# Four late modulation blocks of a two-layer transformer: summed by GpSimd instead of multiplied by TensorE

## The chip, the cores and the metric

The kernel runs on one core of a Trainium2 chip. Its engines are TensorE (PE: matmuls, PEld: its weight loads), VectorE (DVE), ScalarE (ACT), GpSimd (POOL) and SyncE (SP), which here does nothing but start transfers. Each engine takes its own instructions strictly in the order of its program and waits for the others by semaphores. The metric is the device time of one execution in microseconds (us). Times of single instructions are those of the hardware profile.

## What is computed

A stack of two layers over 256 tokens of width 1024, all in float32. Layer 0 mixes with differential attention (8 heads, 256 tokens and 256 context tokens as keys), layer 1 with windowed means; behind each mixer stands a mixture of 32 experts. Both layers are steered by a modulation vector:

```python
c_act = jax.nn.silu(c)
for i in range(DEPTH):
    mod = (c_act @ ada_w[i] + ada_b[i])[:, None, :]
    sh1, s1, g1, sh2, s2, g2 = jnp.split(mod, N_MOD, axis=-1)
    h = modulate(rms_norm(x, norm1_g[i]), sh1, s1)
    ...
    x = x + g1 * y
    h2 = modulate(rms_norm(x, norm2_g[i]), sh2, s2)
    out = moe(h2.reshape(-1, D), router_w, router_b, w_gate[i], w_up[i], w_down[i])
    x = x + g2 * out.reshape(B, L, D)
```

`ada_w` is 2 x 1024 x 6144, so the twelve products of the 1024-vector `c_act` with 1024 x 1024 blocks read 48 MB. Block `i` (0 to 11) is part `i % 6` of layer `i // 6`; blocks 8 to 11 are g1, sh2, s2 and g2 of layer 1, which nothing needs before layer 1's mixer has ended.

## The kernel before

The program is written out by hand, engine by engine, with semaphores; there is no scheduler. The stages around the change, with their times in the profile:

- Blocks 0 and 1 are multiplied by TensorE. Then come ten projections `proj(0)` to `proj(9)` (k, q, v of attention, 16 matmuls each), up to 208 us.
- During them VectorE sums blocks 2 to 7 (`accumulate`, L1120 and L1122): a 4 MB block lies in one of three 32 KB-per-partition buffers, `unit(0)` to `unit(2)`, and eight instructions on 128x1024 add up row k times `c_act[k]`, first one `TENSOR_SCALAR`, then seven `SCALAR_TENSOR_TENSOR`, each linked to the next by a semaphore. TensorE adds over the partitions afterwards (`ada_fin`: eight products of one column, L482, or two of 512 columns with a matrix of ones, L485), at places in the projections that `fin_at` sets: block 6 inside `proj(8)`, block 7 inside `proj(9)`. VectorE takes the result up in `mod_use` and raises `mod_used`.
- Attention runs from 208 to 310 us over 16 units `u` (8 heads times 2 halves of the tokens). Per unit TensorE makes the scores of unit u+2 (L552), transposes the weights of u (L605, `w_ready`) and multiplies them with the values of u-1 (L581); VectorE takes the maxima (L1206, L1207), and mixes the two softmaxes (L1215, L1216, L1219); ScalarE takes the exponentials (L876), copies the transposed weights (L920) and scales the output twice (L910, L913). After every fourth unit VectorE forms a mean square (`squares`, L1225), GpSimd its inverse root (`inverse_root`, a power, L397), VectorE scales the four outputs (`normalise`, L1231, in its program just ahead of the end of u = 5, 9, 13 and after 15), TensorE turns them (`turn_outputs`, L563) and at the end multiplies with `w_out` (`project_outputs`, L587).
- Inside that loop, at u = 0, 2, 6 and 8 (`ADA_AT`), TensorE also multiplies blocks 8 to 11: `ada_mm` (L455, 16 matmuls), with a copy by ScalarE (`mod_copy`, L844) and the fold one unit later (`ada_fin`, L473 or L475).
- SyncE's queue is one list. `load_ada` (L303) brings a block in two halves of 512 columns, `load_rows` (L309) in two halves of 512 rows, so that four k of eight are complete in each. Block 8 is requested when the q projections have freed `unit(1)`, blocks 9 to 11 as TensorE frees a unit, then the weights of experts 0, 2 and 1.
- The experts of layer 0 begin with the first weights at about 362 us and set the pace from there by their loads and matmuls; all that lies behind 310 us follows the last `project_outputs`.

## Time and profile before

| | us |
|---|---|
| three runs | 1396.83, 1392.2, 1397.91; median 1396.83 |
| profiled execution: its own time | 1396.81 |
| profiled execution: span | 1395.0 |
| PE busy (share of the span) | 1231.1 (88%) |
| DVE busy | 390.5 (28%) |
| ACT busy | 214.0 (15%) |
| POOL busy | 70.0 (5%) |
| attention, first transposes to last projection | 210.72 to 310.25 |

The span is the time from the first to the last recorded instruction; 1.8 us lie around it. Busy times overlap and don't add up to the span. For a change inside one stage the shares over the whole program say little: what counts is what the engines wait for in that stage.

### The profile page before, as it was taken

Reading aid. Unit: us, or ns where it says so; the run is one execution under the profiler, and the core shown is the slowest. Engines: PE = TensorE matmul, PEld = TensorE weight load, DVE = VectorE, ACT = ScalarE, POOL = GpSimd, SP = SyncE. Lnnn points to the kernel's source line nnn. Section 1 sums busy time; section 2 is a strip of 40 time slices with the busy share of each in tenths; the row PEclk is TensorE's granted clock in tenths of the full one; section 3 lists DMA queues with packets and bytes.
Section 4 is the critical chain, followed back from the end, with each engine's and each line's share of the span. In section 5 each row is a group of like instructions: output and inputs, shape, how many; then the busy total and the mean of one; then the engine's idle time right before and its main releaser. Section 6 shows DMA issues by size and latency. Waiting matters only on the chain.

```text
span 1395.0 us, 13695 instructions
## 1 busy us (share of the span) xinstructions
PE 1231.1 (88%) x5044; PEld 517.5 (37%) x5048; DVE 390.5 (28%) x834; ACT 214.0 (15%) x449; POOL 70.0 (5%) x86
## 2 busy tenths in 40 slices
PE   4899998885999999798989879679999999898996
PEld 2355444444433333232323257353333333332332
DVE  2665645625321121111111033351111111111112
ACT  3211116611111110100101111111110101001000
POOL 0122100000000000000000000000000000000000
PEclk9999999997999999999999989789999999999999
DMA  9956759443699999999999993537999999999994
GB/s 351 404 203 241 281 202 380 193 199 166 268 421 422 422 422 421 422 422 422 421 421 421 419 380 132 230 120 311 421 422 423 421 422 421 422 422 422 421 422 193
DMA packets 84288, 486.54 MB, mean 349 GB/s; under 512 B 6176, under 2 KB 7712, under 8 KB 35104
## 3 DMA queue, kind: packets, MB, share of 16 engines
q1 hardware_dynamic: 82240, 481.91, 84.7%
q10 hardware_dynamic: 2016, 4.21, 0.9%
q8 instruction: 20, 0.33, 0.1%
q14 instruction: 12, 0.10, 0.0%
HBM read 485.04 MB, written 1.05 MB: 348 GB/s over the span
## 4 chain that ended last, share of the span: by engine, by line
PE 56%; DMA 17%; SPq 14%; DVE 7%; issue 2%; ACT 2%; POOL 1%; another core or an unknown queue 0%; DVEq 0%; POOLq 0%; ACTq 0%
PE PS L678 19%; DMA ring<-in_moe_w_up 14%; PE PS L697 10%; SPq L289 10%; PE PS L527 7%; PE PS L705 4%; SPq L294 3%; DMA ring<-in_ada_w 3%; PE PS L789 2%; PE PS L670 2%; PE PS L807 2%; PE PS L587 2%; PE PS L455 1%; DVE ring L1122 1%; POOL stat L397 1%
## 5 line engine op out<-in xcount | busy, mean ns | idle before, releaser
L678 PE MATMUL PS<-ring,KQH 128*64 128x512 f32 x2048 | 482.7, 615 | 34.3 <-DMA ring<-in_moe_w_up 32.6
L678 PEld LDWEIGHTS PS<-ring,KQH 128*64 128x64 f32 x2048 | 147.2, 141 | 314.9 <-issue 276.8
L697 PE MATMUL PS<-ring,KQH 128*64 128x512 f32 x1024 | 230.7, 592 | 0.9 <-ACT KQH L980 0.9
L1443 DVE COPY TMP<-PS 64x512 f32<-64x512 f32 x64 | 43.8, 684 | 470.8 <-PE PS L697 470.8
L527 PE MATMUL PS<-ring,KQH 128*128 128x512 f32 x320 | 143.0, 604 | 1.5 <-DVE KQH L1139 1.5
L697 PEld LDWEIGHTS PS<-ring,KQH 128*64 128x64 f32 x1024 | 73.7, 137 | 147.1 <-issue 145.7
L705 PE MATMUL PS<-TMP,KQH 128*128 128x512 f32 x256 | 118.4, 605 | 1.6 <-DVE TMP L1443 1.6
L967 ACT COPY TMP<-PS 64x512 f32<-64x512 f32 x64 | 37.2, 582 | 466.4 <-PE PS L697 466.4
L1458 DVE TENSOR_TENSOR KQH<-KQH,PS 128x256 f32<-128x256 f32 x64 | 38.7, 605 | 196.3 <-ACT KQH L986 196.3
L527 PEld LDWEIGHTS PS<-ring,KQH 128*128 128x128 f32 x320 | 61.3, 194 | 75.6 <-issue 72.7
L410 POOL COPY KQH<-KQH 128x512 f32 x62 | 38.2, 616 | 873.5 <-PE PS L678 775.9
L705 PEld LDWEIGHTS PS<-TMP,KQH 128*128 128x128 f32 x256 | 46.0, 189 | 73.6 <-issue 70.3
L1428 DVE TENSOR_SCALAR rope_g<-const,route 128x128 f32<-128x128 f32 x128 | 36.3, 346 | 80.8 <-PE PS L688 80.8
L688 PE MATMUL PS<-const,KQH 128*128 128x128 f32 x128 | 26.3, 287 | 35.8 <-DVE KQH L1458 35.8
L1122 DVE SCALAR_TENSOR_TENSOR ring<-ring,ccols 128x1024 f32<-128x1024 f32 x42 | 54.0, 1285 | 5.6 <-DMA ring<-in_ada_w 4.2
L980 ACT COPY KQH<-PS 128x512 f32<-128x512 f32 x64 | 30.7, 479 | 150.7 <-PE PS L688 150.7
L397 POOL TENSOR_TENSOR stat<-stat,mhalf 128x16 f32<-128x16 f32 (+3 forms) x18 | 31.5, 1752 | 404.9 <-DVE stat L1266 144.0
L986 ACT ACTIVATE KQH<-PS 128x256 f32<-128x256 f32 x62 | 23.8, 384 | 176.8 <-PE PS L678 176.8
L670 PE MATMUL PS<-KQH 128*128 128x256 f32 x128 | 33.9, 427 | 8.3 <-DVE KQH L1370 6.7
L688 PEld LDWEIGHTS PS<-const,KQH 128*128 128x128 f32 x128 | 14.4, 141 | 64.0 <-DVE KQH L1458 64.0
L670 PEld LDWEIGHTS PS<-KQH 128*128 128x128 f32 x128 | 26.3, 215 | 16.1 <-DVE KQH L1370 7.0
L789 PE MATMUL PS<-KQH,ring 128*128 128x256 f32 x128 | 30.4, 403 | 0.7 <-DVE KQH L1276 0.7
(212 smaller groups left out, 732.0 us busy)
## 6 DMA issues: line engine op xcount, KB each, us to landing
ring<-in_moe_w_gate SPq DMA_DIRECT2D x128, 1024.0 KB, 26.8
ring<-in_moe_w_up SPq DMA_DIRECT2D x128, 1024.0 KB, 26.8
ring<-in_moe_w_down SPq DMA_DIRECT2D x64, 2048.0 KB, 28.7
ring<-in_ada_w SPq DMA_DIRECT2D x24, 2048.0 KB, 14.6
ring<-in_attn_w_in SPq DMA_DIRECT2D x2, 4096.0 KB, 13.8
ring<-in_attn_w_in SPq DMA_DIRECT2D x2, 2048.0 KB, 22.0
ring<-in_attn_w_out SPq DMA_DIRECT2D x1, 4096.0 KB, 12.9
ring<-in_pool_w_in SPq DMA_DIRECT2D x1, 4096.0 KB, 26.2
```

Of the source, the lines that this page charges most:

```text
L289: sp.dma_start(gu_w[s][:, a, 4 * part:4 * part + 4, :], w[L.l, e].rearrange("(p k) f -> p k f", p=P)[:, 4 * part:4 * part + 4, :]).then_in ...
L294: sp.dma_start(dn_rows[s], w_down[L.l, e].rearrange("(a p b) n -> p a b n", a=2, b=2)).then_inc(L.dn_in[s], 16)
L397: nc.gpsimd.tensor_tensor(ap, ap, mhalf[:, 0:ap.shape[1]], ALU.pow).then_inc(pow_done, 1)
L527: ins = mm(bank(4 + 2 * (n % 2) + half), hT[:, k, P * t:P * t + P], unit(u)[:, k, 512 * half:512 * half + 512], start=k == 0, stop=k == KC ...
L670: ins = mm(PS[:, b, 0:HALF], xn[:, t, P * k:P * k + P], picked[:, t, :], start=t == 0, stop=t == NT - 1)
L678: ins = mm(PS[64 * f:64 * f + 64, 4, :], xs[:, k, 0:SLOTS], gu_w[s][:, :, k, 256 * f:256 * f + 256], start=k == 0, stop=k == KC - 1)
L688: ins = tr(PS[:, 5, 256 + P * c:256 + P * c + P], h_sb[:, P * c:P * c + P], ident)
L697: ins = mm(PS[64 * f:64 * f + 64, 6, :], lhs, dn_w[s][:, c, 512 * f:512 * f + 512], start=c == 0, stop=c == 3)
L705: mm(bank(2 * t + f), t_sb[:, P * t:P * t + P], y_sb[:, 512 * f:512 * f + 512], start=False, stop=False, skip_group_check=True)
L789: ins = mm(PS[:, 4 + b % 4, 0:256], pool_w[:, k, P * b:P * b + P], h2T[:, k, :], start=k == 0, stop=k == KC - 1)
L1122: ins = V.scalar_tensor_tensor(acc, unit(u)[:, k, :], ccols[:, 32 * k:32 * k + 1], acc, ALU.mult, ALU.add)
L1443: return V.tensor_copy(y_sb[64 * second:64 * second + 64, 0:512], PS[0:64, 6, :])
```

## The change

Blocks 8 to 11 are no longer multiplied by TensorE. All four are loaded by halves of rows into one buffer, `unit(1)`, one half while the other is worked on, and GpSimd sums them: `late_accumulate(i, part)` multiplies four slices of 128x1024 in place by their `c_act[k]` (`tensor_scalar`) and adds them pairwise, into `late_acc` (three adds for part 0, four for part 1). Every instruction whose result the next one reads raises `late_step` and is waited for; a block has seven such steps. TensorE only adds over the partitions (`ada_fin`), at u = 2, 4 and 9 for blocks 8, 9 and 10 and behind the last `turn_outputs` for block 11. ScalarE's copies for them are gone. GpSimd's four inverse roots of attention now stand between the halves of blocks 10 and 11 in its program.

```diff
--- before.py
+++ after.py
@@ -51,9 +51,10 @@
 R_QG, R_KG, R_LQ, R_RB = 0, 64, 128, 384
 N_ROW = 416
 OUT_SCALE = 1 - LAM_INIT
-PE_BLOCKS = (0, 1, 8, 9, 10, 11)
-ADA_AT = {0: 8, 2: 9, 6: 10, 8: 11}
-UNIT_LOADS = ((0, 2, 9, 11), (1, 3, 8, 10), ("k", 4, 5, 6, 7))
+PE_BLOCKS = (0, 1)
+LATE_BLOCKS = (8, 9, 10, 11)
+ADA_AT = {2: 8, 4: 9, 9: 10}
+UNIT_LOADS = ((0, 2), (1, 3, 8, 9, 10, 11), ("k", 4, 5, 6, 7))
 COL_PARTS = (0, 1, 3, 4)
 SPREAD_PARTS = (3, 4)
 SPREAD_COLS = [V_N2, V_N2 + 8] + [V_ADA + 8 * (4 * l + q) for l in range(2) for q in (2, 3)]
@@ -132,7 +133,8 @@
         vals = ring[:, 24576:28672].rearrange("p (t n) -> p t n", t=4)
         work = 28672
         modraw = ring[:, work:work + 1024]
-        acc_of = {5: ring[:, work + 3072:work + 4096], 7: ring[:, work + 5120:work + 6144]}
+        late_acc = ring[:, work + 6144:work + 7168]
+        acc_of = {5: ring[:, work + 3072:work + 4096], 7: ring[:, work + 5120:work + 6144]} | {i: late_acc for i in LATE_BLOCKS}
         raw = ring[:, work + 1024:work + 2048]
         sq = ring[:, work + 2048:work + 3072]
         ra = ring[:, work + 3072:work + 4096]
@@ -241,6 +243,11 @@
         zeroed, minus_half, silu_c, lam_sum, lam_exp = (sem(n) for n in ("zeroed", "minus_half", "silu_c", "lam_sum", "lam_exp"))
         ss_ready, ms_ready, pow_done, xn0_ready = (sem(n) for n in ("ss_ready", "ms_ready", "pow_done", "xn0_ready"))
         mod_mm, mod_raw, mod_fin, mod_used, ada_acc = (sem(n) for n in ("mod_mm", "mod_raw", "mod_fin", "mod_used", "ada_acc"))
+        late_step = sem("late_step")
+
+        def late_steps(i, part):
+
+            return 7 * LATE_BLOCKS.index(i) + (3, 7)[part]
         xt_x, xt_c, h_x, h_c = (sem(n) for n in ("xt_x", "xt_c", "h_x", "h_c"))
         proj_done, proj_used, sq_ready, qn_ready, kq_tr, kq_in = (sem(n) for n in ("proj_done", "proj_used", "sq_ready", "qn_ready", "kq_tr", "kq_in"))
         scored, max_ready, exp_done, w_ready, w_tr, wT_ready, pv_done, o_ready, on_ready, o_tr, oT_ready = (
@@ -330,17 +337,22 @@
                     load_rows(i, part, 2)
                 if i == 5:
                     sp.wait_ge(proj_done, 6)
-                    load_ada(8, 1)
+                    for part in range(2):
+                        load_rows(8, part, 1)
+                if i == 6:
+                    sp.wait_ge(late_step, late_steps(8, 0))
+                    load_rows(9, 0, 1)
             sp.wait_ge(ada_acc, 12)
             sp.dma_start(unit(2), rows_of(w_out[0], 0, D)).then_inc(w_in_s["o"], 16)
+            for i in range(9, 12):
+                for part in range(2):
+                    if (i, part) == (9, 0):
+                        continue
+                    sp.wait_ge(late_step, late_steps(i - 1, part))
+                    load_rows(i, part, 1)
+            L = layers[0]
             sp.wait_ge(proj_done, 10)
-            load_ada(9, 0)
-            sp.wait_ge(mod_mm, 6)
-            load_ada(10, 1)
-            sp.wait_ge(mod_mm, 8)
-            load_ada(11, 0)
-            L = layers[0]
-            sp.wait_ge(mod_mm, 12)
+            sp.wait_ge(late_step, late_steps(11, 0))
             load_expert(L, 0, 0)
             sp.wait_ge(oT_ready, 4)
             sp.wait_ge(mod_used, 12)
@@ -400,8 +412,39 @@
             inverse_root(1, ms0[:, 2:4])
             for n in range(6):
                 inverse_root(2 + n, msk)
-            for g in range(4):
-                inverse_root(8 + g, oms[:, 4 * g:4 * g + 4])
+            steps = [0]
+
+            def step(ins):
+
+                steps[0] += 1
+                ins.then_inc(late_step, 1)
+                pool.wait_ge(late_step, steps[0])
+
+            def late_accumulate(i, part):
+
+                w = [unit(1)[:, 4 * part + k, :] for k in range(4)]
+                pool.wait_ge(unit_in[1][part], 16 * UNIT_LOADS[1].index(i) + 16)
+                for k in range(4):
+                    c = 32 * (4 * part + k)
+                    ins = nc.gpsimd.tensor_scalar(w[k], w[k], ccols[:, c:c + 1], None, ALU.mult)
+                step(ins)
+                nc.gpsimd.tensor_tensor(w[0], w[0], w[1], ALU.add)
+                step(nc.gpsimd.tensor_tensor(w[2], w[2], w[3], ALU.add))
+                if part == 0:
+                    if i > LATE_BLOCKS[0]:
+                        pool.wait_ge(mod_fin, i)
+                    step(nc.gpsimd.tensor_tensor(late_acc, w[0], w[2], ALU.add))
+                else:
+                    step(nc.gpsimd.tensor_tensor(w[0], w[0], w[2], ALU.add))
+                    step(nc.gpsimd.tensor_tensor(late_acc, late_acc, w[0], ALU.add))
+            pool.wait_ge(h_x, KC)
+            g = 0
+            for i in LATE_BLOCKS:
+                for part in range(2):
+                    late_accumulate(i, part)
+                    if i >= 10:
+                        inverse_root(8 + g, oms[:, 4 * g:4 * g + 4])
+                        g += 1
             def windows(L):

                 def window(e, b):
@@ -474,7 +517,10 @@
                         else:
                             ins = mm(bank(half), sel, modraw[:, 512 * half:512 * half + 512], start=True, stop=True)
                 else:
-                    pe.wait_ge(ada_acc, 2 * (i - 1))
+                    if i in LATE_BLOCKS:
+                        pe.wait_ge(late_step, late_steps(i, 1))
+                    else:
+                        pe.wait_ge(ada_acc, 2 * (i - 1))
                     pe.wait_ge(mod_used, i)
                     acc = acc_of.get(i, modraw)
                     if i % 6 in COL_PARTS:
...
@@ -599,7 +642,7 @@
                 pe.wait_ge(w_ready, u + 1)
                 if u >= 1:
                     pe.wait_ge(wT_ready, u)
-                if u in (7, 11):
+                if u in (7, 11, 15):
                     pe.wait_ge(oT_ready, u // 4)
                 for c in range(4):
                     ins = tr(PS[:, 2, P * c:P * c + P], wmix[:, u % 2, P * c:P * c + P], ident)
@@ -609,9 +652,7 @@
                 if u in (6, 10, 14):
                     turn_outputs((u - 6) // 4)
                 if u in ADA_AT:
-                    ada_mm(ADA_AT[u], (1, 0, 1, 0)[ADA_AT[u] - 8])
-                if u - 1 in ADA_AT:
-                    ada_fin(ADA_AT[u - 1])
+                    ada_fin(ADA_AT[u])

             values_product(15)
             for q in range(1, 4):
@@ -621,6 +662,7 @@
                 project_outputs(q)
                 if q == 1:
                     turn_outputs(3)
+                    ada_fin(11)

             def norm_transpose(n):
```

(The last hunks, left out here, only follow from it: ScalarE's `outputs` reads bank 2 always, its `mod_copy` in the loop is gone, and VectorE's `mod_use` stands at u = 2, 4, 9 and behind `normalise(3)`.)

GpSimd's program between its sixth inverse root of the projections and the first one of attention, which followed it at once before (L397 x6, then L397 x4), for block 8 and the end of block 10 after the change (`ring` holds the units and `late_acc`):

```order
L409 TENSOR_TENSOR stat<-stat,mhalf 128x16 x6
L429 TENSOR_SCALAR ring<-ring,ccols 128x1024 x4
L431 TENSOR_TENSOR ring<-ring 128x1024
L432 TENSOR_TENSOR ring<-ring 128x1024
L436 TENSOR_TENSOR ring<-ring 128x1024
L429 TENSOR_SCALAR ring<-ring,ccols 128x1024 x4
L431 TENSOR_TENSOR ring<-ring 128x1024
L432 TENSOR_TENSOR ring<-ring 128x1024
L438 TENSOR_TENSOR ring<-ring 128x1024
L439 TENSOR_TENSOR ring<-ring 128x1024
```

```order
L436 TENSOR_TENSOR ring<-ring 128x1024
L409 TENSOR_TENSOR stat<-stat,mhalf 128x4
L429 TENSOR_SCALAR ring<-ring,ccols 128x1024 x4
L431 TENSOR_TENSOR ring<-ring 128x1024
L432 TENSOR_TENSOR ring<-ring 128x1024
L438 TENSOR_TENSOR ring<-ring 128x1024
L439 TENSOR_TENSOR ring<-ring 128x1024
L409 TENSOR_TENSOR stat<-stat,mhalf 128x4
```

The inverse roots of attention (128x4) now come behind five, six, seven and eight halves of late blocks, of seven and eight instructions each.

SyncE's queue from the loads of blocks 4 and 5 (`proj_done`, `ada_acc`) to the first expert, before:

```order
L303 DMA ring<-in_ada_w 128x8x512 [waits proj_done]
L303 DMA ring<-in_ada_w 128x8x512
L309 DMA ring<-in_ada_w 128x4x1024 [waits ada_acc] x4
L335 DMA ring<-in_attn_w_out 128x8x1024 [waits ada_acc]
L303 DMA ring<-in_ada_w 128x8x512 [waits proj_done]
L303 DMA ring<-in_ada_w 128x8x512
L303 DMA ring<-in_ada_w 128x8x512 [waits mod_mm]
L303 DMA ring<-in_ada_w 128x8x512
L303 DMA ring<-in_ada_w 128x8x512 [waits mod_mm]
L303 DMA ring<-in_ada_w 128x8x512
L289 DMA ring<-in_moe_w_gate 128x2048 [waits mod_mm]
```

and after:

```order
L316 DMA ring<-in_ada_w 128x4x1024 [waits proj_done]
L316 DMA ring<-in_ada_w 128x4x1024
L316 DMA ring<-in_ada_w 128x4x1024 [waits ada_acc] x2
L316 DMA ring<-in_ada_w 128x4x1024 [waits late_step]
L316 DMA ring<-in_ada_w 128x4x1024 [waits ada_acc] x2
L346 DMA ring<-in_attn_w_out 128x8x1024 [waits ada_acc]
L316 DMA ring<-in_ada_w 128x4x1024 [waits late_step] x5
L296 DMA ring<-in_moe_w_gate 128x2048 [waits late_step,proj_done]
```

The first half of block 9 now stands ahead of block 7's two halves, its second half and blocks 10 and 11 behind `w_out`, each behind a step of GpSimd.

TensorE in attention, units 2 and 3 before (L552 scores, L605 transposes, L581 values, L455 and L473 block 9):

```order
L552 MATMUL PS<-KQH 128x512 x2
L605 MATMUL PS<-const,ring 128x128 x4
L581 MATMUL PS<-ring 128x128 x4
L455 MATMUL PS<-ring,ccols 32x512 x16
L552 MATMUL PS<-KQH 128x512 x2
L605 MATMUL PS<-const,ring 128x128 x4
L581 MATMUL PS<-ring 128x128 x4
L473 MATMUL PS<-const,ring 128x128 x8
L552 MATMUL PS<-KQH 128x512 x2
```

and units 3 and 4 after (L598, L648 and L624 are the same three; L528 adds block 9 over the partitions):

```order
L598 MATMUL PS<-KQH 128x512 x2
L648 MATMUL PS<-const,ring 128x128 x4
L624 MATMUL PS<-ring 128x128 x4
L598 MATMUL PS<-KQH 128x512 x2
L648 MATMUL PS<-const,ring 128x128 x4
L624 MATMUL PS<-ring 128x128 x4
L528 MATMUL PS<-const,ring 128x1 x8
```

Sixteen products of 512 columns and eight transposes a block have become eight products of one column (blocks 9 and 10) or two of 512 columns (8 and 11).

## Rows read from the trace of the kernel before

**Rows 1.** The page of the profiled execution: its span.

```profile
span 1395.0 us, 13695 instructions
```

**Rows 2.** The chain that ended last, in order of time: start us, us, what.

```profile
208.14 17.49 DMA ring<-in_ada_w
...
252.59 3.57 PE PS L455 x32
...
296.25 13.98 PE PS L587 x32
```

**Rows 3.** Timeline, TensorE's transposes of units 0, 11, 14 and 15: start us, us.

```profile
210.72 0.66 PE L605 MATMUL PS<-const,ring 128*128 128x128 f32 x4
...
266.36 0.63 PE L605 MATMUL PS<-const,ring 128*128 128x128 f32 x4 [1.31 <-ACT KQH L883]
...
275.45 0.66 PE L605 MATMUL PS<-const,ring 128*128 128x128 f32 x4 [1.68 <-DVE ring L1219]
...
284.55 0.60 PE L605 MATMUL PS<-const,ring 128*128 128x128 f32 x4
```

**Rows 4.** One stretch of attention: busy us of each engine, TensorE's granted clock.

```profile
209.00:236.00 27.00, 24.26 (x158) 11.45 (x157) 15.33 (x30) 14.91 (x43) 0.00 (x0) 1.00 1.02 374
```

**Rows 5.** What ScalarE waited for from 205 to 312: us, times, longest.

```profile
ACT ring L876 <- DVE stat L1207: 7.0, 9, 2.7
```

**Rows 6.** Groups of GpSimd's instructions, whole program: busy us, mean ns.

```profile
L410 POOL COPY KQH<-KQH 128x512 f32 x62 | 38.2, 616 | 873.5 <-PE PS L678 775.9 <-ACT KQH L962 49.7 <-issue 47.7
L397 POOL TENSOR_TENSOR stat<-stat,mhalf 128x16 f32<-128x16 f32 x6 | 22.8, 3803 | 112.7 <-DVE stat L1152 112.7
L397 POOL TENSOR_TENSOR stat<-stat,mhalf 128x4 f32<-128x4 f32 x4 | 4.0, 1009 | 135.4 <-DVE stat L1225 135.4
L397 POOL TENSOR_TENSOR stat<-stat,mhalf 128x1 f32<-128x1 f32 x6 | 3.3, 544 | 144.0 <-DVE stat L1266 144.0
```

**Rows 7.** Two lines of VectorE: duration ns min/median/max, first and last start.

```profile
L1468 DVE TENSOR_SCALAR route<-route x30: 158/534/553, 359.9 to 1334.0; 128x4 f32<-128x4 f32 x30
...
L1428 DVE TENSOR_SCALAR rope_g<-const,route x128: 332/341/782, 348.8 to 1338.1; 128x128 f32<-128x128 f32 x128
```

**Rows 8.** Timeline of GpSimd and VectorE around one of those L1468.

```profile
412.55 0.61 POOL L410 COPY KQH<-KQH 128x512 f32 x1 [11.39 <-PE PS L678]
412.66 0.53 DVE L1468 TENSOR_SCALAR route<-route 128x4 f32<-128x4 f32 x1
```

**Rows 9.** Timeline around one of the six powers of 16 columns.

```profile
64.73 1.22 DVE L1158 TENSOR_TENSOR ring<-ring,rope_g 128x1024 f32<-128x1024 f32 x1
64.90 3.81 POOL L397 TENSOR_TENSOR stat<-stat,mhalf 128x16 f32<-128x16 f32 x1 [49.71 <-DVE stat L1152]
...
65.86 1.30 DVE L1161 TENSOR_TENSOR ring<-ring,rope_g 128x512 f32<-128x512 f32 x2
```

**Rows 10.** Timeline of VectorE: the sums of blocks 5, 6 and 7.

```profile
152.98 9.21 DVE L1122 SCALAR_TENSOR_TENSOR ring<-ring,ccols 128x1024 f32<-128x1024 f32 x7
...
171.00 5.25 DVE L1122 SCALAR_TENSOR_TENSOR ring<-ring,ccols 128x1024 f32<-128x1024 f32 x4 [1.73 <-DMA ring<-in_ada_w]
...
183.97 5.25 DVE L1122 SCALAR_TENSOR_TENSOR ring<-ring,ccols 128x1024 f32<-128x1024 f32 x4 [1.97 <-DMA ring<-in_ada_w]
```

**Rows 11.** Timeline of SyncE: block 8, w_out.

```profile
143.24 0.99 SPq L303 DMA_DIRECT2D ring<-in_ada_w  x2
...
189.24 0.37 SPq L335 DMA_DIRECT2D ring<-in_attn_w_out  x1
```

**Rows 12.** Issue to landing of block 8's two halves, then of w_out.

```profile
DMA to landing us min/median/max: 7.9/10.4/12.9
...
DMA to landing us min/median/max: 12.9/12.9/12.9
```

**Rows 13.** Timeline of TensorE: block 6 and block 7 are added over the partitions.

```profile
180.84 1.84 PE L482 MATMUL PS<-const,ring 128*128 128x1 f32 x16
...
198.89 1.84 PE L482 MATMUL PS<-const,ring 128*128 128x1 f32 x16
```

More of the change, by code:

```diff
@@ L557, in turn_outputs @@
                 pe.wait_ge(on_ready, g + 1)
-                if g >= 2:
-                    pe.wait_ge(mod_used, 12)
-                else:
-                    pe.wait_ge(wT_ready, 4 * g + 7)
+                pe.wait_ge(wT_ready, min(4 * g + 7, 16))
                 for j in range(4):
-                    ins = tr(PS[:, (2, 2, 0, 1)[g], P * j:P * j + P], o_sb[:, 4 * (g % 2) + j, :], ident)
+                    ins = tr(PS[:, 2, P * j:P * j + P], o_sb[:, 4 * (g % 2) + j, :], ident)
                 ins.then_inc(o_tr, 1)
@@ L883, in outputs @@
                 A(oT[:, 4 * (g % 2):4 * (g % 2) + 4, P * (g // 2):P * (g // 2) + P],
-                  bank((2, 2, 0, 1)[g]).rearrange("p (j n) -> p j n", j=4), ACT.Identity,
+                  bank(2).rearrange("p (j n) -> p j n", j=4), ACT.Identity,
                   scale=vec[:, V_SUB:V_SUB + 1]).then_inc(oT_ready, 1)
@@ L920, in _ @@
                 nc.scalar.copy(wT[:, u % 2].rearrange("p c n -> p (c n)"), bank(2)).then_inc(wT_ready, 1)
-                if u - 1 in ADA_AT:
-                    mod_copy(ADA_AT[u - 1])
                 if u < 14:
@@ L1245, in _ @@
                     normalise(u // 4 - 1)
-                if u - 1 in ADA_AT:
-                    mod_use(ADA_AT[u - 1])
+                if u in ADA_AT:
+                    mod_use(ADA_AT[u])
             squares(3)
             normalise(3)
+            mod_use(11)
             def residual(g, first, wait):
```

## The prediction, made before the changed kernel ran

> **What bounds the kernel now.** The page gives the frame: a span of 1395.0 us in a profiled execution of 1396.81, so 1.8 us lie around it [rows 1]; the median of the three runs is 1396.83, the same number. I read the chain that ended last between 205 and 310 us next, since the edited part lies there. It shows three things of the edit on the chain itself: 17.49 us from the request of block 9 to its products at 225.68, and 3.57 us of products of block 11, as of block 10 before it [rows 2]. Attention is thus partly spent on blocks that nothing needs yet. The stretch from 209 to 236 has TensorE busy 24.26 of 27 us at the full granted clock (2.4 GHz) [rows 4]. The timeline gives the pace: unit 0's transposes at 210.72, unit 11's at 266.36, unit 14's at 275.45, unit 15's (behind the first output projection) at 284.55 [rows 3]. Units 11 to 14 have no block product beside them and take (275.45 - 266.36) / 3 = 3.04 us each. At that pace TensorE waits for VectorE and ScalarE in turn; the maxima's scaling L1207 releases ScalarE's exponentials in nine of the units [rows 5], so what delays VectorE there delays the unit. From 284.55 to the end of the last projection at 310.25 it is 25.7 us [rows 2, 3], and the rest of the program follows rigidly. The last of the early expert loads is requested then; its 6 MB take some 15 us at 5.0 us per 2 MB [rows 12], and the first expert's products come some 50 us behind the projections, before and after, so the expert loads cost nothing.
>
> **What it removes.** Without blocks, unit 14 would start near 210.7 + 14 x 3.04 = 253.3. What stays beside the units costs: the product with ones of block 8 and its 1.2 us addition on VectorE about 1.5, blocks 9 and 10 about 1.8 each (eight one-column products, 1.84 [rows 13]), three turns of outputs some 0.6 each. So 260, against 275.45: 15 us to gain if GpSimd were free. At the end block 11's products add 1.3 between `turn_outputs(3)` and the projection, partly in a gap of 0.9 that is there now.
>
> **What GpSimd's work costs.** No row has the added operations. The nearest for `tensor_scalar` 128x1024 is the copy of 128x512 at 0.616 us [rows 6]: between 0.62 and 1.23 if nothing is fixed; I take 1.2. The `tensor_tensor` reads two tensors, so between that 1.23 and twice it, 2.46; I take 2.3. The power rows (0.544, 1.009 for 1 and 4 columns [rows 6], 0.155 a column) bound nothing near, being a computed function; as far end I take double my values. A half alone is then 4 x 1.2 + 3 x 2.3 + 0.4 for the step waits = 12.1 us, with four adds 14.5. Four blocks need 106 us. They can begin at 143.24 + 7.9 = 151.1, block 8's landing [rows 11, 12].
>
> **Do VectorE and GpSimd hold each other up?** This decides the sign. L1468, four columns, takes 158 ns alone and 534 ns at the median; in the timeline 28 of the 30 lie under a GpSimd copy of 0.61 and end with it [rows 7, 8], and L1428 takes up to 782 instead of 341 [rows 7]. So GpSimd does hold such instructions of VectorE. For instructions with two SBUF inputs, as the sums L1122 and the mix L1219, there is one trace: the power takes 0.155 us a column, so 16 columns should take 1.009 + 12 x 0.155 = 2.87, and take 3.80 in all six cases [rows 6]; each began 0.17 us after a two-input VectorE instruction of 1.22 us [rows 9]. The excess of 0.93 is about what that one still had to run, 1.05. I read that as GpSimd held until it ended. The L1161 pair of 512 columns inside the same power ran unhindered, 1.30 for both [rows 9], so the hold covers the reading, not a whole instruction.
>
> The Trainium skill, SBUF — State Buffer, section "Who interferes with whom", says that a VectorE instruction with two SBUF inputs contends with a GpSimd instruction that reads SBUF, and that the first holds the shared ports for its whole instruction. The rows agree that they contend and not that it is for the whole instruction; by the page's length of hold, each pair below would cost some 0.4 us more, and the sum some 8 us more. Its GPSIMD Engine Reference, section 3.1, has 4.5 us for an add of 2048 columns; halved, an estimate of 2.25 for ours, which no row here shows and which would leave the sum as it is.
>
> **The projections.** Blocks 5, 6 and 7 are summed from 152.2 on by eight instructions each of 1.3 us (7 in 9.21 [rows 10]) while GpSimd works on block 8 and half of 9. If they alternate, a pair costs both streams less some 0.4 of fixed parts that overlap: 2.1 with a `tensor_scalar`, 3.2 with an add, 2.6 on the mean of GpSimd's mix. A block then takes 20.8 instead of 10. Block 5 ends at 173 instead of 162.2. Block 6, whose second half is requested then and lands by 182, ends at 193.5 instead of 176.25. Block 7 has GpSimd beside it only in its first half and ends at 212 instead of 189.2. TensorE wants block 6 at 180.84 and block 7 18 us later [rows 13]; it stops until 193.5, so unit 0 is at 210.72 + 12.7, say 224.
>
> **Attention.** SyncE's queue has `w_out` behind block 7, and the second half of block 9 behind that, whose buffer GpSimd freed long ago. It is requested at 212, not 189.2 [rows 11], and lands after `w_out`'s 12.9 and 5.0 more (the distance of the two halves' landings, 12.9 against 7.9 [rows 12]): 230. From there GpSimd never rests. Each unit's mix takes the port for some 0.5, three units a half, so halves take 13.6 and 16. Half (9,1) is done at 246, (10,0) at 259.6 and the first inverse root, 1.0 [rows 6], at 260.6; (10,1) at 276.6, root 277.6; (11,0) at 291.2, root 292.2; (11,1) at 308, root 309. On the other side each unit has two VectorE instructions (L1207, L1219) that may meet a GpSimd instruction in flight and wait on average half of one, 0.7 each: 4.4 a unit. From 224, unit 4 is at 243; block 9 is waited for until 246. VectorE stops at its u = 5 for the first root; behind that instruction stand all later maxima, so everything stops until 260.6. Unit 6 at 262, unit 9 at 275.5, block 10 waited for until 276.6, unit 10 at 281, unit 14 at 299 (its root is there at 292), unit 15 at 308, end 308 + 25.7 + 1.3 = 335 against 310.25. That is 24.7 slower: 1396.8 + 24.7 = 1421.5, and I say 1421. Where GpSimd reads as fast as a copy for both kinds (1.2 and 1.2), the same steps give block 7 at 200, unit 0 at 216, roots at 240, 253 and 264, unit 15 at 287, end 314: 1401. The case's own range is 1401 to 1440.
>
> **The rivals.** (1) Same place, no hold between two-input instructions and GpSimd, only L1207's: the excess of the power would then have another cause, such as its arithmetic. Projections stay as they are, (9,1) lands at 207.4 (189.2 + 0.4 + 17.8), roots at 235, 251 and 264; units at 3.04 + 0.7 to 0.9 reach unit 6 at 237, unit 14 at 271, unit 15 at 281, end 308: -2, 1395. (2) Faster: no wait on the path at all, GpSimd and VectorE fit between one another. Unit 6 waits for the root until 236, unit 9 for block 10 until 250, unit 14 is at 266, end 302.4: -8, 1389. It ends on the other side and decides if the two-input sums L1122 keep their 1.285 us beside GpSimd. For it speaks that L1161 ran undisturbed; against it stand the excess of the power and what L1468 shows [rows 6 to 8]. (3) GpSimd's instructions take up to double: five halves stand between 230 and the root of u = 13, so each us more per half adds some 4; at double it is +66, 1463; at a fifth more, 1432. (4) TensorE, idle for 12 us before 193.5, is granted 1.2 GHz for a while. It adds 2 to 3 us ahead of unit 0, and nothing to the end, since unit 6 waits for GpSimd; it is inside the range.
>
> **How the numbers follow.** The forecast's case 0.60; rival 1 0.15; rival 2 0.15; rival 3 0.10. A measurement of this kernel tells about 0.5% (7 us) from no change. Faster than 1389.8: most of rival 2 and a little of rival 1, 0.18. Within: rival 1 and the rim of the forecast's case, 0.13. Slower: 0.69. The range must take in part of the faster case to leave out no more than 2 in 10: 1388 to 1440.
>
> **What would show it.** In the changed profile the sums of blocks 5 to 7 should average over 2 us instead of 1.285, unit 0's transposes should lie near 224, VectorE should wait for GpSimd's power ahead of unit 6 for some 8 us, and GpSimd's adds should take 2 to 3 us. If L1122 keeps 1.285, the forecast is wrong and rival 1 or 2 holds, told apart by the units' pace: 3.9 or 3.1 us. If the first root of attention is there before VectorE asks, GpSimd is quicker than I took it.

## The result and the profile after

The changed kernel takes 1441.42 us (median of 4 runs, 1438.87 to 1442.16) against 1395.76 us for the kernel before (4 runs, 1392.2 to 1397.91): a ratio of 1.0312, interval [1.0288, 1.0336]. It is 3% slower. The direction is the one forecast; the time lies 20 us above the 1421 said, and 1.4 us over the range's top of 1440. In the experiments below one execution (1532.38 us, with two buffers) fell in a slow state of the chip, with a granted clock of 0.87, and is left out of its median (1433.79 us; 1436.29 with it).

The page of the changed kernel; the third and fourth lines are slices of 36 us each:

```profile
span 1439.3 us, 13530 instructions
PE 1236.5 (86%) x4932; PEld 528.1 (37%) x4936; DVE 428.5 (30%) x832; ACT 210.1 (15%) x441; POOL 238.5 (17%) x146
...
POOL 0122896994000000000000000000000000000000
PEclk9999998679799999999999999969999999999999
```

The span is 44.3 us longer than before [rows 1]. GpSimd is busy in slices 5 to 10, where the kernel before has 1 in slice 5 and 0 behind it, and nowhere new after them. The last projection now ends at 355.29 instead of 310.25, which is 45.0 us: the whole loss arises before that point, and the rest of the program follows rigidly.

The changed kernel's groups by line, VectorE and then GpSimd, from 148 to 360 us; and one line's instructions with their shortest, median and longest duration in ns:

```profile
L1162 DVE SCALAR_TENSOR_TENSOR ring<-ring,ccols 128x1024 f32<-128x1024 f32 x21 | 44.6, 2126 | 0.7
L1259 DVE SCALAR_TENSOR_TENSOR ring<-ring,stat 128x512 f32<-128x512 f32 x16 | 19.7, 1230 | 0.6
L1246 DVE TENSOR_REDUCE stat<-PS 128x2 f32<-128x1024 f32 x16 | 19.5, 1221 | 13.6 <-PE PS L598 13.3
L1247 DVE TENSOR_SCALAR stat<-stat 128x2 f32<-128x2 f32 x16 | 7.8, 486 | 0.5
...
L429 POOL TENSOR_SCALAR ring<-ring,ccols 128x1024 f32<-128x1024 f32 x32 | 97.3, 3055 | 0.9 <-DMA ring<-in_ada_w 0.5
L432 POOL TENSOR_TENSOR ring<-ring 128x1024 f32<-128x1024 f32 x8 | 20.6, 2576 | 0.0
```
```profile
L429 POOL TENSOR_SCALAR ring<-ring,ccols x32: 2837/2842/3695, 152.1 to 324.8; 128x1024 f32<-128x1024 f32 x32
```

For comparison the same view of the kernel before:

```profile
L1122 DVE SCALAR_TENSOR_TENSOR ring<-ring,ccols 128x1024 f32<-128x1024 f32 x21 | 27.0, 1285 | 4.4 <-DMA ring<-in_ada_w 3.7
L1219 DVE SCALAR_TENSOR_TENSOR ring<-ring,stat 128x512 f32<-128x512 f32 x16 | 12.0, 752 | 0.6
L1207 DVE TENSOR_SCALAR stat<-stat 128x2 f32<-128x2 f32 x16 | 2.7, 169 | 0.6
```

Above all three VectorE instructions stretch beside GpSimd: the sums (1285 to 2126 ns), the mixes (752 to 1230) and the two-column scalings (169 to 486 on the mean; most stay at 171, the longest takes 1370). The four-column scaling in front of each root goes from 170 to 1606. The maxima's reduction, which reads PSUM only, stays at 1221. And a GpSimd multiplication takes 2.84 us, not 1.2.

The timeline of GpSimd in the changed kernel, around blocks 9 and 10:

```profile
200.36 12.71 POOL L429 TENSOR_SCALAR ring<-ring,ccols 128x1024 f32<-128x1024 f32 x4
213.16 2.34 POOL L431 TENSOR_TENSOR ring<-ring 128x1024 f32<-128x1024 f32 x1
215.46 2.34 POOL L432 TENSOR_TENSOR ring<-ring 128x1024 f32<-128x1024 f32 x1
229.14 2.36 POOL L436 TENSOR_TENSOR ring<-ring 128x1024 f32<-128x1024 f32 x1 [11.34 <-PE PS L531]
231.60 11.30 POOL L429 TENSOR_SCALAR ring<-ring,ccols 128x1024 f32<-128x1024 f32 x4
...
271.05 1.04 POOL L409 TENSOR_TENSOR stat<-stat,mhalf 128x4 f32<-128x4 f32 x1
272.08 11.83 POOL L429 TENSOR_SCALAR ring<-ring,ccols 128x1024 f32<-128x1024 f32 x4
...
337.33 1.04 POOL L409 TENSOR_TENSOR stat<-stat,mhalf 128x4 f32<-128x4 f32 x1
```

GpSimd never rests from 229.14 to the last root but for moments. The one pause lies before that and is 11.34 us long: block 9's first write to `late_acc` waits until TensorE has folded block 8 out of the same 1024 columns, which `ADA_AT` places at unit 2. Then come the waits of TensorE (150 to 360 us: total, times, longest) and the stretches of time (us, PE busy, PEld, DVE, ACT, POOL, granted clock as a share of 2.4 GHz, DMA share, GB/s):

```profile
PE PS L528 <- POOL ring L439: 23.0, 2, 17.5
PE PS L606 <- DVE ring L1271: 8.9, 1, 8.9
PE PS L648 <- DVE ring L1259: 8.3, 5, 2.5
```
```profile
221.00:260.00 39.00, 19.98 (x96) 13.28 (x97) 15.22 (x29) 12.80 (x39) 30.42 (x12) 0.71 0.45 167
260.00:290.00 30.00, 16.13 (x74) 10.21 (x73) 15.93 (x21) 11.07 (x34) 29.60 (x13) 0.75 0.19 71
290.00:320.00 30.00, 20.56 (x95) 15.75 (x96) 22.97 (x33) 13.65 (x41) 29.51 (x13) 0.71 0.33 120
```

TensorE waits for GpSimd's sums (23.0 us), for the normalisation behind a root (8.9) and for the mixes (8.3), some 40 us in place of the 2.3 it waited for mixes before. From 221 to 260 it is busy 20 of 39 us; in the kernel before it was busy 24.26 of 27 between 209 and 236, at the full clock [rows 4]. Now, with these pauses, it is granted 0.71 to 0.75 on the mean, a mixture of its two levels (1.2 and 2.4 GHz).

### The profile page after: what moved, and what is told of

The parts are those of the page before. It is cut to its first block, busy times and chain, and to the rows that moved or that the text cites. A ratio compares the mean times of both kernels' runs of the same rounds, so it can differ in the third digit from the quotient of the medians.

```text
span 1439.3 us, 13530 instructions
## 1 busy us (share of the span) xinstructions
PE 1236.5 (86%) x4932; PEld 528.1 (37%) x4936; DVE 428.5 (30%) x832; ACT 210.1 (15%) x441; POOL 238.5 (17%) x146
## 4 chain that ended last, share of the span: by engine, by line
PE 52%; SPq 15%; DMA 14%; DVE 9%; POOL 6%; issue 3%; ACT 2%; another core or an unknown queue 0%; DVEq 0%; POOLq 0%
PE PS L720 19%; DMA ring<-in_moe_w_up 12%; SPq L296 11%; PE PS L739 10%; PE PS L573 5%; PE PS L747 5%; SPq L301 3%; POOL ring L429 2%; DVE ring L1162 2%; PE PS L712 2%; DMA ring<-in_ada_w 2%; PE PS L630 2%; PE PS L831 2%; PE PS L849 2%; POOL stat L409 1%
## 5 line engine op out<-in xcount | busy, mean ns | idle before, releaser
L573 PE MATMUL PS<-ring,KQH 128*128 128x512 f32 x320 | 146.4, 615 | 1.6 <-DVE KQH L1179 1.5
L429 POOL TENSOR_SCALAR ring<-ring,ccols 128x1024 f32<-128x1024 f32 x32 | 97.3, 3055 | 0.9 <-DMA ring<-in_ada_w 0.5
L573 PEld LDWEIGHTS PS<-ring,KQH 128*128 128x128 f32 x320 | 62.4, 198 | 78.3 <-issue 74.7
L1162 DVE SCALAR_TENSOR_TENSOR ring<-ring,ccols 128x1024 f32<-128x1024 f32 x42 | 71.6, 1705 | 1.9 <-DMA ring<-in_ada_w 0.5
L528 PE MATMUL PS<-const,ring 128*128 128x1 f32 x96 | 20.1, 340 | 27.3 <-POOL ring L439 23.0
```

The lines of the kernel that those rows point to most:

```text
L429: ins = nc.gpsimd.tensor_scalar(w[k], w[k], ccols[:, c:c + 1], None, ALU.mult)
L573: ins = mm(bank(4 + 2 * (n % 2) + half), hT[:, k, P * t:P * t + P], unit(u)[:, k, 512 * half:512 * half + 512], start=k == 0, stop=k == KC ...
L1162: ins = V.scalar_tensor_tensor(acc, unit(u)[:, k, :], ccols[:, 32 * k:32 * k + 1], acc, ALU.mult, ALU.add)
```

## The experiments

Theory A at this point: what costs is GpSimd's chain of halves, for which attention waits. Theory B: what costs is that GpSimd and VectorE hold each other, wherever the waits are. The runs take them apart. All times are medians; the kernel before was run beside each group of them, and took 1395 to 1397 us. Every ratio is against it.

### Two buffers for the sums

```diff
-        acc_of = {...} | {i: late_acc for i in LATE_BLOCKS}
+        acc_of = {...} | {i: (late_acc, modraw)[i % 2] for i in LATE_BLOCKS}
```
with L436's wait for the fold of the block before last in place of the last.

> Blocks 8 and 10 are summed in one buffer, 9 and 11 in a second (modraw), so the last add of (9,0) no longer waits for block 8's fold on TensorE. Theory A (the chain of GpSimd's halves sets the end of attention): GpSimd's 11.3 us of idling at 217.8 vanish and all later gates come 11 us earlier, 1441.4 - 11 = 1430. Theory B (the holds between VectorE and GpSimd set the pace, GpSimd's chain only runs beside it): 1441 as before. Theory C (TensorE's low granted clock costs it): 1441 less at most 2.

1433.79 us (3 runs), ratio 1.0275 [1.0227, 1.0322]: 5 to 8 us less than the changed kernel, by ratio or by median, with intervals that overlap; not the 11 of the pause. GpSimd's timeline in this run says why:

```profile
217.67 2.34 POOL L437 TENSOR_TENSOR ring<-ring 128x1024 f32<-128x1024 f32 x1
227.62 11.75 POOL L430 TENSOR_SCALAR ring<-ring,ccols 128x1024 f32<-128x1024 f32 x4 [7.61 <-DMA ring<-in_ada_w]
```

The fold no longer stops it, but block 9's second half lands only now, since it is requested behind `w_out`, and `w_out` behind block 7's sum. One wait hid another; the chain of halves goes on 4 us earlier.

### GpSimd begins behind VectorE's last sum

```diff
             pool.wait_ge(h_x, KC)
+            pool.wait_ge(ada_acc, 12)
```
and block 9's first half is requested behind `w_out`.

> GpSimd begins block 8 only when VectorE has summed block 7 (ada_acc 12), and block 9's first half is requested behind w_out. Theory A: the sums of blocks 5 to 7 return to 1.285 us an instruction and unit 0 to about 211 us, but block 8 is worked on from 190 to 230 instead of 152 to 200, (9,0) ends at 248 instead of 231.5, and the rest shifts with it: 1441 + 17 = 1458. Theory B: 9 us of the projections come back and nothing else changes, 1432.

1454.5 us, ratio 1.0416 [1.0375, 1.0456]. VectorE's sums are at 1285 ns again and unit 0 is at 211.45, within 0.7 us of where it was before the change: the projections' loss is the hold. But the four roots come at 288, 311, 332 and 354 instead of 271, 294, 315 and 337, and TensorE waits 45.6 us for GpSimd's sums: 37.3 in two waits for blocks 9 and 10, and 8.3 for block 8. The time is near theory A's 1458. Undoing the hold where it is cheap moved the chain where it is dear.

### Multiplications in another form

```diff
-  ins = nc.gpsimd.tensor_scalar(w[k], w[k], ccols[:, c:c + 1], None, ALU.mult)
+  ins = nc.gpsimd.tensor_tensor(w[k], w[k], ccols[:, c:c + 1].broadcast_to([P, D]), ALU.mult)
```

> The 32 multiplications on GpSimd are written as tensor_tensor with the column of c_act broadcast over 1024 columns. If such an instruction costs what the adds do (2.34 us) instead of 2.84, four halves between 229 us and the third root save 2 us each, and by theory A the time is 1441 - 8 = 1433. By theory B 1441 or a little more, since a second input meets VectorE's reads oftener. If the broadcast reads slower, over 1441 by theory A, 4 x 4 us for each us more.

1450.54 us, ratio 1.0396 [1.0359, 1.0433]: slower than the changed kernel by 9 us, although each multiplication became shorter (four in 7.44 to 8.34 us in attention, 11.3 before). VectorE in this run, 148 to 360 us:

```profile
L1162 DVE SCALAR_TENSOR_TENSOR ring<-ring,ccols 128x1024 f32<-128x1024 f32 x21 | 56.8, 2703 | 0.7
L1259 DVE SCALAR_TENSOR_TENSOR ring<-ring,stat 128x512 f32<-128x512 f32 x16 | 26.3, 1643 | 0.6
```

The sums went from 2126 to 2703 ns. The form with two operands holds VectorE more than the form with one operand and a column, so unit 0 came at 236 instead of 219.

### The instructions kept, their work taken away

```diff
-                w = [unit(1)[:, 4 * part + k, :] for k in range(4)]
+                w = [unit(1)[:, 4 * part + k, 0:8] for k in range(4)]
```
so that GpSimd works on 8 of 1024 columns, and blocks 8 to 11 are not computed.

> GpSimd's 60 late instructions work on 8 columns of 1024 instead of all, so blocks 8 to 11 of the modulation are not computed; loads, semaphores, folds and order stay. Theory A: with GpSimd's time gone the kernel is left with what the edit removes from TensorE, 15 us less 1.3: about 1383, the sums of blocks 5 to 7 at 1.285 us. Rival: taking the products off TensorE frees nothing, since the units wait for each other anyway: 1396. If the loads' new order costs by itself, above 1396.

1387.58 us, ratio 0.9947 [0.9921, 0.9972], between the 1383 of theory A and the 1396 of the rival. This is the change with GpSimd almost for free, the loads in their new order, and it gains 7 to 8 us only; the last projection ends at 303.3, against 310.25. So the new order of the loads isn't what costs. The run also shows the hold from the other side. GpSimd's timeline beside VectorE's sums and without them:

```profile
157.76 5.30 POOL L430 TENSOR_SCALAR ring<-ring,ccols 128x8 f32<-128x8 f32 x4
163.15 0.20 POOL L432 TENSOR_TENSOR ring<-ring 128x8 f32<-128x8 f32 x1
```

Four tiny multiplications take 1.33 us each while VectorE sums in instructions of 1.285 us, one behind the other; 163.15 lies in a gap of VectorE, and an addition of 8 columns takes 0.20 there. So GpSimd gets in between two of VectorE's instructions and not during one. The Trainium skill, SBUF — State Buffer, section "Who interferes with whom", says just that of the shared ports (whoever is first holds them for the whole instruction); these rows agree for VectorE's side, on which the prediction had GpSimd held until VectorE's instruction ended, too.

For GpSimd's side the rows of the changed kernel don't agree with it. The chain that ended last shows single sums, the first two beside a multiplication of GpSimd, the third beside an addition:

```profile
155.96 2.03 DVE ring L1162
158.02 1.30 DVE ring L1162
168.85 3.26 DVE ring L1162
```

Beside multiplications every other sum or so takes 2.03 us and the rest 1.30, so a multiplication of 2.84 us delays VectorE by 0.73 only. An addition, 2.34 us alone, delays it by 1.96. Neither holds it for the whole instruction.

### Additions and memsets beside the sums, in the kernel before

```diff
+            for n in range(16):
+                pool.wait_ge(dummy, n + 1)
+                nc.gpsimd.tensor_tensor(dum, dum, dum, ALU.add).then_inc(dummy, 1)
```
(`dum` is 1024 free columns, `dummy` a semaphore of its own.)

> The kernel before with 16 additional GpSimd additions of two 128x1024 operands (in place, on a free area of the buffer), from about 145 us on, while VectorE sums the modulation blocks; their results aren't used. It measures the hold by itself, without any use of GpSimd's sums. If what stretches VectorE's two-input sums beside GpSimd is GpSimd's reading of two operands: the sums of 128x1024 that lie beside the additions take over 2 us (1.285 us before), the additions 2.3 to 3.5 us each, and the projections end 8 to 15 us later, the kernel at 1403 to 1410. Rival (the stretch comes from the shared buffer and its waits, not from a port): sums at 1.285 us and the kernel within 3 us of 1395.

The second kernel has `nc.gpsimd.memset(dum, 0.0)`, 40 times.

> The kernel before with 40 additional GpSimd memsets of 128x1024 in the same place as the additions of the run beside it. A memset only writes. If reading is what counts: VectorE's sums stay at 1.285 us and the time within 3 us of 1395. If any GpSimd instruction on the buffer holds VectorE: the sums over 1.7 us and the kernel 5 us or more later.

One run each: 1418.62 us with additions, 1396.81 with memsets; 1395.46 for the kernel before, whose runs lie between 1388.73 and 1402.36. VectorE and GpSimd, first with additions, then with memsets:

```profile
L1130 DVE SCALAR_TENSOR_TENSOR ring<-ring,ccols 128x1024 f32<-128x1024 f32 x21 | 48.2, 2293 | 2.6 <-DMA ring<-in_ada_w 1.8
...
L410 POOL TENSOR_TENSOR ring<-ring 128x1024 f32<-128x1024 f32 x16 | 42.1, 2634 | 1.3
```
```profile
L1130 DVE SCALAR_TENSOR_TENSOR ring<-ring,ccols 128x1024 f32<-128x1024 f32 x21 | 27.0, 1285 | 4.0 <-DMA ring<-in_ada_w 3.3
...
L410 POOL MEMSET ring<- 128x1024 f32 x40 | 39.4, 984 | 2.3
```

GpSimd is busy for some 40 us in both. Where it reads, VectorE's sums take 2293 ns, unit 0 comes at 232.6 instead of 210.7 and the kernel takes 23 us more, well over what I had expected. Where it only writes, the sums stay at 1285 ns and the time is within the spread of the kernel before. For the sums it is the reading. (The same section of the Trainium skill says that an instruction of GpSimd that only writes doesn't contend with one of VectorE that has two inputs in SBUF; this agrees.) The one-input product at the head of each sum does feel the memsets: L1128 takes 1089 ns on the mean of three, 750 in the kernel before.

### Additions beside attention, in the kernel before

The same additions, 27 of them, from unit 0's scores (about 193 us) on, between the four roots.

> The kernel before with 27 additional GpSimd additions of 128x1024 from unit 0 on, between its roots; their results aren't used, and TensorE keeps its four late blocks. It asks whether GpSimd beside the attention units costs time by itself, where nothing waits for its sums. If VectorE's two-input mixes (128x512, 0.75 us before, 1.23 in the changed kernel) are held: mixes at 1.1 to 1.4 us, TensorE waits for them 8 us or more (2.3 before) and the kernel at 1403 to 1412. Rival (TensorE is busy enough with its own products to cover the mixes): under 1399.

1410.75 us, ratio 1.0099 [1.0068, 1.0131]. Nothing waits for these additions, each root finds GpSimd idle for 10 us or more, and 13 us are gone. The mixes, from 200 to 345 us, and TensorE's wait for them:

```profile
L1228 DVE SCALAR_TENSOR_TENSOR ring<-ring,stat 128x512 f32<-128x512 f32 x16 | 20.2, 1261 | 0.6
```
```profile
PE PS L614 <- DVE ring L1228: 8.4, 4, 4.5
```

8.4 us where the kernel before has 2.3. VectorE's scaling of the outputs stretches too (L1240, 686 to 1956 ns). The granted clock falls with it, 0.91 from 221 to 260 and 0.86 from 260 to 290 (1.00 before), and TensorE's own products take longer.

### The waits placed otherwise

```diff
-ADA_AT = {2: 8, 4: 9, 9: 10}
+ADA_AT = {2: 8, 6: 9, 14: 10}
...
-                    if i >= 10:
+                    if (i, part) in ((9, 1), (10, 0), (10, 1), (11, 0)):
```
with the two buffers, and block 11's fold behind the last projection. GpSimd's work is the same.

> The changed kernel with the same work on GpSimd, the waits placed otherwise: two buffers for sums instead of one, each block's root one half earlier in GpSimd's queue, the folds of blocks 8, 9 and 10 at units 2, 6 and 14, block 11's fold behind the last projection's start. If the loss is due to where attention waits for GpSimd's chain: 1412 to 1420, the waits of TensorE for GpSimd under 10 us in all (23.0 in the changed kernel). If it is the length of the chain of halves itself, whatever the placement: 1432 to 1438, as with two buffers alone (1436.3).

1423.49 us, ratio 1.0192 [1.0149, 1.0236]: 18 us less than the changed kernel, 3.5 above the range of the first expectation and 8.5 below the second's. The wait L676 lies behind the last projection and is there before, too (5.3 us). The waits of TensorE, and its stretches:

```profile
PE PS L649 <- DVE ring L1261: 14.6, 8, 3.7
PE PS L676 <- DVE KQH L1311: 6.5, 1, 6.5
PE PS L607 <- DVE ring L1273: 6.1, 1, 6.1
...
PE PS L532 <- POOL ring L440: 1.9, 1, 1.9
```
```profile
221.00:260.00 39.00, 28.27 (x136) 19.37 (x136) 23.97 (x44) 20.12 (x62) 31.97 (x13) 0.76 0.43 167
260.00:290.00 30.00, 20.85 (x102) 13.51 (x101) 26.85 (x30) 15.64 (x47) 29.43 (x13) 0.78 0.20 71
```

23.0 us of waiting for sums have become 1.9, and yet the kernel is 28 us slower than before. The wait for the mixes took their place, 14.6 us. The placement, theory A's part, accounts for 18 of the 46 us; most of the other 28 are theory B's by the rough account below.

### Block 8 on VectorE instead

The kernel before, with `PE_BLOCKS = (0, 1, 9, 10, 11)` and `accumulate(8, 1)` behind block 7; block 9 is requested once 8 is summed.

> The kernel before with block 8 alone taken from TensorE: VectorE sums it behind block 7, in the gap it has there (the trace of before shows it idle), and TensorE makes 9, 10 and 11 as before. If what is to be gained is TensorE's time for a late block (4 products' worth, 3.5 to 7 us a block) and what cost in the change is GpSimd: 1388 to 1391, a ratio near 0.995 to 0.997. Rival (attention waits for VectorE in that stretch, or the requests move against the loads): 1395 or more.

1390.71 us (12 runs), ratio 0.9967 [0.9944, 0.999]: a gain of some 4.6 us, small, with no change just outside the interval. VectorE is busy 4.2 of the 22 us from 189 to 211 in the kernel before, and sums the block there at 1285 ns an instruction; TensorE has 3.7 us of products less (a quarter of the 14.8 that the four late blocks' products took), and the last projection ends at 303.9. (The profiled execution, 1385.75, was the fastest of the twelve.) It is the fastest version but for the one that leaves the blocks out.

### Two further versions of it

Block 9 on VectorE too, two instructions in each of units 2 to 5:

> The last candidate (VectorE sums block 8) with block 9 on VectorE too, two instructions of 1.285 us in each of units 2 to 5. If TensorE's time is what bounds the attention stage: another 3 us off, 1386 to 1389. Rival (an added 2.6 us a unit on VectorE makes TensorE wait for the mixes): 1391 or more.

1399.74 us (12 runs), ratio 1.0024 [1.0004, 1.0044]. The rival holds: VectorE is no longer in a gap there, and TensorE waits for it; block 9's fold, of one-column products, takes another 3.78 us between the units.

```profile
PE PS L607 <- DVE ring L1226: 7.3, 6, 2.0
```

Block 11 alone on GpSimd, begun at 210:

> The last candidate (VectorE sums block 8) with block 11 alone on GpSimd, begun behind VectorE's last sum, its roots between the halves' instructions so that none is late. GpSimd works 42 us of the attention stage. If the hold of the mixes and the lower clock eat what TensorE saves (3.7 us of products): no gain over the candidate, 1390 to 1396. Rival (what cost was the chain of eight halves alone, one block is free): 1386 to 1388.

1404.76 us (12 runs), ratio 1.0049 [1.0028, 1.007], 14 us above the version with block 8 alone (some 11 by the ratios, since the kernel before was 2 us slower beside this one), and more than the 1396 I allowed. In this run the mixes, and what TensorE waits for:

```profile
L1259 DVE SCALAR_TENSOR_TENSOR ring<-ring,stat 128x512 f32<-128x512 f32 x16 | 17.7, 1107 | 0.6
```
```profile
PE PS L640 <- DVE ring L1259: 7.5, 5, 2.7
...
PE PS L520 <- POOL ring L419: 4.9, 1, 4.9
```

Even one block costs more than TensorE saves by it, 3.7 us. Part of the loss is my placement, the 4.9 us above all: its queue had GpSimd wait 11.6 us for each of two roots' inputs, so the block was late.

## Why the prediction was right, and where it was off

**The sign was right, and for the reasons given.** The sums L1122 average over 2 us, as said (2.126, forecast 2.6). The adds take 2.34 us (2.3 taken). Attention stands still until the first root, and that root is late: 271.1 against 260.6. That (9,1) starts at 231.6, near the 230 said, is luck: its request came at 207.2 and not at 212, and what held it last was the fold of block 8 (below), not its landing. The runs show the mechanism: sums at 1285 ns with memsets or with GpSimd begun later, 2293 with additions.

**The term that was mis-sized: the multiplication of 128x1024.** I took 1.2 us from the copy of 128x512, with double as the far end; it takes 2.84, over twice. A half by itself, four multiplications in 11.3 us and three adds of 2.34, is thus 18.3 us and not 12.1. With VectorE beside it the halves from 252.54 on take 18.4 and 21.9 where I had 13.6 and 16. By the step of rival 3, "each us more per half adds some 4" (there are four halves from (9,1) to the third root, not five as it says), 5 us more a half is 20 us: 1421 + 20 = 1441. The rival was right in size, and I gave it 1 in 10, since a copy seemed the same kind of instruction. It isn't: the multiplication by a column costs more than an addition of two tensors. That the sum meets the measured time to the microsecond is luck, since the errors below, in both directions, aren't in it.

**The projections were taken too dear**: unit 0 at 218.9, not 224, so 8.2 us and not 13. I had one sum to each GpSimd instruction, 2.1 us a pair with a multiplication and 3.2 with an addition. Beside multiplications the two don't alternate: about two sums fit beside one, and a sum takes 1.63 us (7 in 11.41, block 5). Beside additions it takes 2.83 (7 in 19.79 in the run that adds one tensor to itself) to 3.26. I had block 6 at 193.5; it ended at 184.2, and TensorE stopped 3.5 us for it. Another 2.7 us of the 8.2 are products of the next half that took 9.77 instead of 7.11 at the lower clock, near the 2 to 3 of point (4).

**The length of the hold** I read as shorter than the whole instruction, from L1161 inside a power of GpSimd. It is so for GpSimd's instructions, which delay a sum by 0.73 us of 2.84 (multiplication) and 1.96 of 2.34 (addition). VectorE's two-operand instructions hold for their whole length, as I read from the power's excess: beside them GpSimd starts one 8-column instruction a sum.

**Not foreseen: the fold of block 8.** I let (9,0) end freely and had GpSimd wait for the landing of (9,1) alone. The shared `late_acc` stopped it for 11.3 us. Since the landing holds it until 227.6 in any case, as the run with two buffers shows, it cost some 4 us.

**Taken too large: the gain with GpSimd free.** I had 15 us; with 8 columns it is 7 at the last projection, 7 to 8 in time. Half of the 8 that are missing is the price of the folds of blocks 9 and 10, eight one-column products each (16 in the traces). I took 1.84 us from blocks 6 and 7 [rows 13]. But `by_column` takes the columns of parts 3 and 4 with a step of 8, and 9 and 10 are such parts, as 3 and 4 are. Block 3's fold in the kernel before, and block 9's in the run with 8 columns:

```profile
87.75 3.94 PE PS L482 x16
```
```profile
227.25 3.86 PE L529 MATMUL PS<-const,ring 128*128 128x1 f32 x16
```

Block 4's takes 3.73 in the kernel before, so the rows for the right price were there; the two folds together cost 4.0 us more than I took. It isn't the clock: it was granted in full from 249 to 253, in block 10's fold of the run with 8 columns, which also takes 3.86. The step is what the dear folds have in common (blocks 3, 4, 9 and 10) and the cheap ones lack (6 and 7); no run changes it alone. The other half is clock: behind each of the two folds of that run the granted clock falls to 0.50, and is 0.87 from 221 to 260. The value products L625 of that run take 19.2 us where the kernel before has 17.3 for as many, the scores 17.1 against 15.3, the transposes 11.1 against 10.4. I had said that the low clock adds nothing in attention. With all waits placed better (1423.49) the value products, scores, transposes, turns and output projections sum to 86.9 us, against 78.3 in the run with 8 columns for the same products: 8.6 us, which I put down to the clock, 0.73 to 0.78 from 221 to 320.

**The account of the 45 us at the last projection.** 8.2 before unit 0; 18 for the placement of waits (1441.4 less 1423.5, with the buffer's); some 13 for the hold in attention, by the additions in the kernel before; 8.6 for the clock; less 7 gained. That is 41. These terms were measured in different kernels, and the clock's overlaps the hold's, so the match is rough and an estimate, and what the remaining 4 us are stays open.

## What to carry to other kernels

Work that leaves the busiest engine isn't free on an idle one that shares SBUF reads with a third: ask what that third engine does meanwhile, and who waits for it. Here an empty gap of VectorE was worth 4.6 us, and work on an idle GpSimd beside a busy VectorE cost 13 even where nobody waited for its results. An operation that no row shows should be bounded by a test of its own form, since a copy said nothing of a multiplication by a column; one that rows do show is priced by the rows with its own access pattern (columns with a step of 8, not contiguous ones); and two waits in a row hide each other, so removing the visible one gives back only its lead over the next.

## What the runs showed of the hardware

- GpSimd, 128x1024 float32: multiplication by a column 2.84 us; the same as a two-operand product with the column broadcast 1.86 to 2.09; addition of two tensors 2.34; memset 0.98. The shorter form of the product is the one that holds VectorE more.
- Beside additions of one tensor to itself (1.89 us at the shortest) a VectorE sum takes 2.83 us, less than the 1.285 + 1.89 = 3.18 of strict turns. Beside a multiplication by a column it takes 1.30 or 2.03, beside an addition of two tensors 3.26, beside memsets 1.285 as alone. So the part of a GpSimd instruction that VectorE waits for depends on its form: 0.73 of 2.84 us for the multiplication by a column, 1.96 of 2.34 for the addition.
- The folds of sixteen one-column products whose weights lie at a step of 8 columns take 3.7 to 4.0 us (blocks 3 and 4 before, 9 and 10 after), those with contiguous weights 1.84 (blocks 6 and 7 in the kernel before).
- The granted clock fell to 0.71 to 0.75 where TensorE paused for GpSimd's sums and VectorE's mixes, but to 0.87 too from 221 to 260 in the run with 8 columns, where no wait for GpSimd was left: it stood at 0.50 from 231 to 237 and from 255 to 257, each time behind a fold of one-column products with that step. In the kernel before it is 0.50 from 135 to 137 behind the same kind of fold, of block 4. With block 8 on VectorE, whose fold has no one-column products, it stayed at 1.00 from 211 to 290.
